# Two transformer blocks on one core: conditioning slots on other hosts, opening transfers reordered, second-half low parts on GpSimd

## What is computed

```python
# first block, for each of 2 layers
mod = silu(c) @ w_ada + b_ada                      # conditioning: 3 x 1024 values
shift, scale, gate = split(mod, 3)
h = rmsnorm(x, norm_g) * (1 + scale) + shift
rq, rk, rv, rg, xbc, dt, z, fq, fk, fv, fg, f = split(h @ w_in)
ret = rmsnorm(retention(rotary(rq), rotary(rk), rv)) * silu(rg)
xs, B, C = split(silu(causal_conv4(xbc)))
y = ssd_scan(xs, softplus(dt + dt_bias), -exp(a_log), B, C)    # then gated by z and normed
fox = causal_attention(fq, fk, fv, cumsum(log_sigmoid(f)))     # then gated by fg
x = x + gate * (concat(y, ret, fox) @ w_out)

# second block, for each of 2 layers, on latent and context positions (2 x 256; layer 1: latent only)
mod_x, mod_c = silu(c) @ ada_w + ada_b, silu(c_ctx) @ ada_w + ada_b     # 6 x 1024 values each
h = rmsnorm(x) * (1 + sc1) + sh1
conv = swish(layernorm(dwconv31(a * sigmoid(g)))) @ w_conv_out          # a, g: cua, cug
mlstm = bidirectional chunked mLSTM(mq, mk, mv, gates mg), normed, gated by mo, @ w_mlstm_out
att = grouped-query attention(aq, ak, av) @ w_attn_out
x = x + g1 * ((sigmoid(bg0) * conv + sigmoid(bg1) * mlstm + sigmoid(bg2) * att) @ w_out)
h = rmsnorm(x) * (1 + sc2) + sh2
u = dwconv3(h @ w_up)                                                   # upa, upg: 22 tiles each
x = x + g2 * ((u_a * silu(u_g)) @ w_down)
```

## Time and profile before

| | before |
|---|---|
| median of 3 runs | 2320.07 us |
| the profiled execution | 2319.95 us (span 2318.2 us) |
| PE busy | 2220.0 us, 96% |
| DVE busy | 1677.5 us, 72% |
| ACT busy | 978.7 us, 42% |
| POOL busy | 107.8 us, 5% |
| mean granted clock of TensorE | 0.983 |
| read from HBM | 321.29 MB |

### The profile page before, as it was taken

The page is one execution under the profiler, slowest core; times in us unless marked ns, Lnnn a source line. Parts: engine busy times, 40 slices in busy tenths (PEclk is TensorE's granted clock), DMA queues, the critical chain, the costliest instruction groups (busy, mean ns, idle before and its releaser), DMA issues.

```text
span 2318.2 us, 33297 instructions
## 1 busy us (share of the span) xinstructions
PE 2220.0 (96%) x13838; PEld 1886.0 (81%) x13838; DVE 1677.5 (72%) x3037; ACT 978.7 (42%) x1568; POOL 107.8 (5%) x86
## 2 busy tenths in 40 slices
PE   4999998999999999999999999999999999999999
PEld 3888887988877887778887677866778888998999
DVE  5897749877779776648734699976377767666984
ACT  3347643486523354453222333321244445644542
POOL 0000000000000022220000000000000222100000
PEclk9999999999999999999999999999999999999999
DMA  9883247533343111115522355544532212564553
GB/s 358 281 291 125 93 145 239 182 112 107 110 165 91 55 56 52 41 37 182 163 95 89 105 183 182 188 154 154 175 94 73 92 55 74 173 209 145 183 173 119
DMA packets 280807, 324.49 MB, mean 140 GB/s; under 512 B 28496, under 2 KB 261456, under 8 KB 280528
## 3 DMA queue, kind: packets, MB, share of 16 engines
q1 hardware_dynamic: 280656, 322.36, 42.3%
HBM read 321.29 MB, written 1.05 MB: 139 GB/s over the span
## 4 chain that ended last, share of the span: by engine, by line
PE 76%; DVE 18%; ACT 2%; DMA 2%; issue 1%; SPq 0%; POOL 0%; DVEq 0%; ACTq 0%
PE ps L732 74%; DVE ring L1886 3%; DVE parts L1928 2%; DVE ada_dot L1886 2%; DVE parts L2294 2%; DMA ring<-w_in 1%; DVE arena L2323 1%; ACT w_high L1390 1%; DVE arena L2657 1%; DVE arena L2659 1%; DVE arena L2027 1%; PE ps L1181 1%; DVE arena L2480 1%; DMA cols<-columns 1%; DVE arena L2072 0%
## 5 line engine op out<-in xcount | busy, mean ns | idle before, releaser
L732 PE MATMUL ps<-parts,w_high 128*128 128x256 f32 (+1 forms) x6512 | 1160.5, 328 | 12.8 <-issue 9.6
L732 PEld LDWEIGHTS ps<-parts,w_high 128*128 128x128 f32 x6512 | 977.6, 191 | 138.1 <-issue 24.3
L732 PE MATMUL ps<-parts,parts 128*128 128x256 f32 (+1 forms) x3384 | 618.3, 324 | 22.4 <-DVE parts L2294 11.9
L732 PEld LDWEIGHTS ps<-parts,parts 128*128 128x128 f32 x3384 | 507.4, 191 | 84.7 <-DVE parts L2294 17.3
L1390 ACT ACTIVATE w_high<-ring 128x1024 fp32r<-128x1024 f32 (+2 forms) x442 | 439.4, 1011 | 304.3 <-PE ps L732 171.7
L2294 DVE TENSOR_TENSOR parts<-ring,w_high 128x1024 fp32r<-128x1024 f32 (+2 forms) x282 | 320.5, 1142 | 141.4 <-ACT w_high L1390 141.1
L1886 DVE CUSTOM_DVE_ANT_0 ring<-ring,c_rows,cols 128x1024 f32<-128x1024 f32 x144 | 183.1, 1279 | 19.1 <-DMA ring<-w_ada_t 10.2
L732 PE MATMUL ps<-arena 128*64 128x256 f32 (+7 forms) x928 | 184.2, 396 | 11.3 <-ACT arena L1471 8.4
L1831 POOL TENSOR_TENSOR parts<-ring,w_high 128x512 fp32r<-128x512 f32 x80 | 107.4, 1368 | 1871.8 <-ACT w_high L1390 1871.7
L732 PEld LDWEIGHTS ps<-arena 128*128 128x128 f32 (+2 forms) x928 | 122.5, 171 | 59.5 <-issue 19.8
L2323 DVE SCALAR_TENSOR_TENSOR arena<-arena,cols 128x512 f32<-128x512 f32 (+1 forms) x240 | 159.5, 664 | 6.2
(11 more groups left out here) (266 smaller groups left out, 1854.7 us busy)
## 6 DMA issues: line engine op xcount, KB each, us to landing
ring<-w_in SPq DMA_DIRECT2D x118, 1024.0 KB, 5.1
ring<-ada_w_t SPq DMA_DIRECT2D x48, 1024.0 KB, 4.9
ring<-ffn_w_up SPq DMA_DIRECT2D x44, 1024.0 KB, 5.0
ring<-w_ada_t SPq DMA_DIRECT2D x24, 1024.0 KB, 7.0
ring<-w_out SPq DMA_DIRECT2D x16, 1024.0 KB, 5.1
ring<-ffn_w_down SPq DMA_DIRECT2D x16, 1024.0 KB, 5.3
ring<-w_out SPq DMA_DIRECT2D x16, 512.0 KB, 4.2
ring<-w_mlstm_out SPq DMA_DIRECT2D x8, 1024.0 KB, 5.1
```

The costliest lines, as they stand in the source:

```text
L732: return tensor.matmul(o, a, b, start=first, stop=last)
```

## The change

Five things are changed.

1. Other hosts (`conditioning_slots`). In the first block rv 1 of layer 0 becomes a host, xbc 0, 2 and 4 are no longer, and the first two slots of the output projection become hosts. In layer 1 the eight hosts are rv 1, fv 0, fv 1, rq 1, rk 1, fq 0, fk 0 and a slot of the output projection (before: rq 0 and xbc 1 in place of fk 0 and the last). In the second block the six slots of the conv and mLSTM projections that were hosts are none any more; nine bg and three bo slots carry what these and six bg slots carried. In the feed-forward stage the same twenty slots ride on upa and upg, but each step gets one with four tile products (on upg) and, but for two steps, one with two (on upa).
2. The opening: rv 0 is loaded ahead of the last two of the eight first conditioning slots; small and positions, the conditioning slot of rv 1 and rv 1 follow, and then the other parameter columns, constants and vectors. The waits for the other columns move to where they are read.
3. fv 0's tiles are computed ahead of the dt chain (in both layers).
4. The low parts of the second halves of rq, rk, xbc, fq and fk are computed by GpSimd (`one_lows`), 14 a layer, each as two instructions.
5. `weights_low_out` computes tiles of a host.

```diff
+FIRST_AHEAD = 6
 def conditioning_slots():
-    host(named(0, ("fv", 2), ("rq", 2), ("rk", 2), ("xbc", 6), ("fq", 2), ("fk", 2)), slots[1, 0][8:] + slots[1, 1])
-    host([("rv", 1, 1), ("fv", 1, 0), ("fv", 1, 1), ("rq", 1, 0), ("rq", 1, 1), ("rk", 1, 1), ("xbc", 1, 1), ("fq", 1, 0)], slots[2, 0][:8])
-    host([("cua", 0, 0), ("cug", 0, 1), ("cua", 0, 1), ("mk", 0, 0), ("mk", 0, 1), ("mk", 0, 2)], slots[2, 0][8:14])
-    host([("bg", 0, 0, 3)] + [("bg", 0, 1, s) for s in range(4)] + [("bg", 0, 2, 0)], slots[2, 0][14:20])
-    host([(part, 0, s) for s in range(1, 11) for part in ("upa", "upg")], slots[2, 0][20:] + slots[2, 1][:16])
+    odd = [("xbc", 0, s) for s in (1, 3, 5)]
+    host([("rv", 0, 1)] + named(0, ("fv", 2), ("rq", 2), ("rk", 2)) + odd + named(0, ("fq", 2), ("fk", 2)) + [("wo", 1, 0, s, 0) for s in range(2)],
+         slots[1, 0][8:] + slots[1, 1])
+    host([("rv", 1, 1), ("fv", 1, 0), ("fv", 1, 1), ("rq", 1, 1), ("rk", 1, 1), ("fq", 1, 0), ("fk", 1, 0), ("wo", 1, 1, 2, 0)], slots[2, 0][:8])
+    gates = [("bg", 0, n // 4, n % 4) for n in range(GATES_WHOLE, 12)]
+    host(gates + [("bo", 0, 2, s) for s in range(3)], slots[2, 0][8:20])
+    host([("upg", 0, s) for s in range(1, 11)], slots[2, 0][20:] + slots[2, 1][:6])
+    late = slots[2, 1]
+    host([("upa", 0, s) for s in range(1, 11)], late[8:10] + late[6:7] + late[10:13] + late[7:8] + late[13:16])
...
     first, hosts = conditioning_slots()
-    for slot in first:
+    main = main_slots(w)
+    for slot in first[:FIRST_AHEAD]:
         yield conditioning(slot)
-    for name, parts in main_slots(w):
+    yield next(main)
+    for slot in first[FIRST_AHEAD:]:
+        yield conditioning(slot)
+    for name, parts in main:
...
+SHARED_LOWS = ("rq", "rk", "xbc", "fq", "fk")
...
             load("c_row", c_row[:, 0, :], w["c_row"][0:1, :].to_broadcast([P, D]), "c_row")
+            load_slot(0)
             load("consts", cst[:, 0:N_FIRST], w["shape_consts"][:, 0:N_FIRST], "cst")
             load("row_0", cols[:, 1, :], w["columns"][:, 1, :], "row_0")
-            load_slot(0)
             load_slot(1)
             load("x_in", xT, w["x_t"], "x_in")
-            for n in range(2, RING):
+            for n in range(2, len(ada_first) + 1):
+                load_slot(n)
+            load("small", smalls[:, :], w["small"])
+            load("small", posi, w["positions"][0:1, :].to_broadcast([P, SEQ]), "small")
+            first_main = len(ada_first) + 1
+            for n in range(first_main, first_main + 2):
                 load_slot(n)
             load("rows", cols[:, 0, :], w["columns"][:, 0, :])
             load("rows", cols[:, 2:, :], w["columns"][:, 2:, :], "rows")
-            for n in range(RING, len(ada_first)):
-                load_slot(n)
-            load("small", ...)
-            load_slot(len(ada_first))
...
@@ GpSimd
+            def one_lows(l):
+                for n in range(half_no[("rq", l, 0), 0], half_no[("fk", l, 1), 1] + 1):
+                    (name, j), nk = split_halves[n], KT // 2
+                    if name[0] in SHARED_LOWS and j:
+                        p.wait_ge(*when(("w_high", n)))
+                        for part in (slice(0, nk), slice(nk, KT)):
+                            gpsimd.tensor_tensor(half_low(n)[:, part, :], half_raw(n)[:, part, :], half_high(n)[:, part, :].bitcast(F32), ALU.subtract).then_inc(*p.step(("w_low", n)))
+            for l in range(DEPTH):
+                one_lows(l)
@@ VectorE, weights_low
                         ada_tiles((part, l, s), j)
+                        if j and part in SHARED_LOWS:
+                            continue
...
-                ada_tiles(("rv", l, 1), 0)
-                ada_tiles(("rv", l, 1), 1)
+                for host in (("rv", l, 1), ("fv", l, 0)):
+                    ada_tiles(host, 0)
+                    ada_tiles(host, 1)
                 v.wait_ge(*when(("logs", l)))
...
-                for s in range(2):
-                    for j in range(2):
-                        ada_tiles(("fv", l, s), j)
+                ada_tiles(("fv", l, 1), 0)
+                ada_tiles(("fv", l, 1), 1)
...
                 def weights_low_out(n):
                     n += half_no[("wo", 1, l, 0, 0), 0]
+                    ada_tiles(*split_halves[n])
```

More of the change, by code:

```diff
@@ L197, in conditioning_slots @@
     named = lambda l, *parts: [(part, l, s) for part, n in parts for s in range(n)]
-    host(named(0, ("fv", 2), ("rq", 2), ("rk", 2), ("xbc", 6), ("fq", 2), ("fk", 2)), slots[1, 0][8:] + slots[1, 1])
-    host([("rv", 1, 1), ("fv", 1, 0), ("fv", 1, 1), ("rq", 1, 0), ("rq", 1, 1), ("rk", 1, 1), ("xbc", 1, 1), ("fq", 1, 0)], slots[2, 0][:8])
-    host([("cua", 0, 0), ("cug", 0, 1), ("cua", 0, 1), ("mk", 0, 0), ("mk", 0, 1), ("mk", 0, 2)], slots[2, 0][8:14])
-    host([("bg", 0, 0, 3)] + [("bg", 0, 1, s) for s in range(4)] + [("bg", 0, 2, 0)], slots[2, 0][14:20])
-    host([(part, 0, s) for s in range(1, 11) for part in ("upa", "upg")], slots[2, 0][20:] + slots[2, 1][:16])
-    host([("down", 0, s, part) for s in range(1, 4) for part in range(3)][:8], slots[2, 1][16:])
+    odd = [("xbc", 0, s) for s in (1, 3, 5)]
[7 more added lines that the diff above has]
+    host([("upa", 0, s) for s in range(1, 11)], late[8:10] + late[6:7] + late[10:13] + late[7:8] + late[13:16])
+    host([("down", 0, s, part) for s in range(1, 4) for part in range(3)][:8], late[16:])
     return first, hosts
@@ L688, in _ @@
             load("rows", cols[:, 2:, :], w["columns"][:, 2:, :], "rows")
-            for n in range(RING, len(ada_first)):
-                load_slot(n)
-            load("small", smalls[:, :], w["small"])
-            load("small", posi, w["positions"][0:1, :].to_broadcast([P, SEQ]), "small")
-            load_slot(len(ada_first))
             load("consts_2", cst[:, N_FIRST:], w["shape_consts"][:, N_FIRST:])
@@ L697, in _ @@
                 load("c_rows", c_row[:, vector, :], w["c_row"][vector:vector + 1, :].to_broadcast([P, D]), "c_rows")
-            for n in range(len(ada_first) + 1, len(slots)):
+            for n in range(first_main + 2, len(slots)):
                 if slots[n][0] == ("wo", 1, DEPTH - 1, 3, 1):
@@ L1405, in first_layer @@
                     scalar.activation((xconv if l else h1)[:, t, :], xT[:, t, :], ACT.Square).then_inc(*a.step(("sq1", l, t)))
-                if l == 0:
-                    a.wait_ge(*when("rows"))
                 rms_root(("ssq1", l), rms1[:, 0:SEQ // 4], D, ("root1", l), 0, SEQ // 4)
@@ L1418, in first_layer @@
                     scalar.activation(sinT, sinT, ACT.Sin).then_inc(*a.step("rope"))
+                    a.wait_ge(*when("rows"))
                 for s in range(2):
@@ L1914, in first_layer @@
                 v.wait_ge(*when("x_in"))
-                v.wait_ge(*when("rows"))
                 for t in range(KT):
@@ L1934, in first_layer @@
                     v.wait_ge(*when("small"))
+                    v.wait_ge(*when("rows"))
                     v.wait_ge(*when("cst"))
```

## The result

The changed kernel takes 2304.66 us (median of 9 runs, 2303.21 to 2316.18), the kernel before 2320.57 (9 runs beside them): ratio 0.995 with an interval of 0.9937 to 0.9964, so 0.5% faster and clear of no change. (The medians alone lie 0.7% apart; the ratio counts all runs, and the means are 2308.1 and 2320.5.) Six of the nine runs lie between 2303.2 and 2307.0 at a mean granted clock of 0.984 to 0.987, three between 2314.2 and 2316.2 at 0.978 and 0.979; the profiled one took 2306.98 (span 2305.2), 13.0 us of span less than the one before. The forecast was 2303. The total was met, but not by the steps that were to give it.

A forecast was written before the change was run, and what follows sets the result against it. TensorE, busy 2220.0 of 2318.2 us, was taken as the bound, waiting mainly for VectorE. First block's front and rq to fk -7.9, Part 4 -7.9, Part 5 -3.5, Part 6 +2.0: -17.3 from 2320.07, so 2303 us, range 2296 to 2310.

The forecast's parts named there:

- Part 1: Opening up to rq in layer 0: rq starts 5.2 us earlier, at 67.8 us (bounds 0 and 6).
- Part 2: rq to fk, layer 0: VectorE takes 77.5 us plus 28 GpSimd instructions' cost; the end comes at 170.5 us (-3.1).
- p: VectorE time lost per GpSimd instruction in rq to fk: taken as 0.9 us, bounds 0 to 1.40.
- Part 3: rq to fk, layer 1: VectorE 70.9 us of work plus 6 idle, plus GpSimd's cost; end at 454.0 us (-4.8).
- third rival: rq to fk: each GpSimd subtraction stops VectorE for its whole length; 2322 or 2331 us, chance 0.12.
- Part 4: Second block's conv and mLSTM projections: six hosts removed, TensorE's waits go, -7.9 us (bounds 0 and -9.6); branch stage 0.
- Part 5: Feed-forward of layer 0: heavy and light slots alternate, 6 tiles per step instead of 8; -3.5 us (bounds -2 and -3.5).
- Part 6: Output projection, both layers: added hosts cost +2 us (bounds 0 and +4), 1.2 in layer 0 and 0.8 in layer 1.
- The clock: Second block's projections: lower clock after the long wait, 0.77 granted in 730 to 740 us, 2.3 us of work.
- free GpSimd: rq to fk: GpSimd costs VectorE nearly nothing and TensorE is the bound in both layers; 2283 us, chance 0.25.
- stalls that return: Second block: stalls return elsewhere, branch stage delayed, feed-forward stays VectorE-bound; 2313 us, chance 0.13.
- the port rival: Same as the third rival: VectorE stopped throughout each GpSimd subtraction in rq to fk; 2322 or 2331 us, chance 0.12.

The follow-up runs named there:

- e4: Kernel before with only the new opening load order and fv 0's tiles ahead of the dt chain in both layers: 2310.18 us, ratio 0.996.
- e9: Kernel after with no rq-to-fk low parts on GpSimd, no conditioning slot ahead of rv 1, layer 0's hosts shifted later, last in output projection's fifth half: 2281.95 us.
- e2: Kernel before with only the 28 low parts of rq to fk moved to GpSimd: 2344.64 us, ratio 1.0109.
- e1: Kernel after with all low parts of rq to fk back on VectorE, the rest unchanged: 2292.13 us, ratio 0.9875.
- e10: Kernel after with the tiles of two layer 1 conditioning slots moved from fv 1 and rq 1 to xbc 1 and xbc 3: 2308.45 us, ratio 0.9958.
- e3: Kernel before with only the second block's hosts changed: 2301.77 us, ratio 0.993.

## Why the prediction was right in the sum and wrong in its parts

**Part 1, the front:** the order of events was right, one term mis-sized. "TensorE then needs 14.08 us for both fv slots": it took 15.57 at a lowered clock, and began at 54.95 instead of 53.2. With the full clock, and with one conditioning slot less ahead of it, rq starts at 67.75 (e4). "rq 0 has landed by then" was wrong too: the DMA queue delivered it at 68.2, behind one more conditioning slot; in the kernel after both limits lie close together, and e9 shows that taking away that slot alone gains nothing.

**Part 2, layer 0:** right. Forecast 77.5 + 25.2 = 102.7 us for the stretch, measured 103.0 (70.17 to 173.18); p forecast at 0.9 from the convolution steps of the second block, measured 0.89. The end is 2.7 us late, mostly because rq started 2.4 us late. "The moved subtraction thus saves 1.14 us and costs 1.8 us of the same engine" is what e2 and e1 show: 10 us more for layer 0 with the move alone, 10 less without it.

**Part 3, layer 1:** this step failed. VectorE's price was even lower than forecast (0.70), and TensorE was rid of the 5.42 us. But "with 6 us of idling as in layer 0" had VectorE idle for 6 us and it idled for 20.1: TensorE waited for GpSimd, the high-part buffers stayed full, and VectorE had nothing to do (7.74 us in one piece up to 377.24). So the stretch took 110.2 us in place of 102.1, 14.1 more of idling and 6.1 less of work; it also began 2.6 us later than forecast. I had asked what GpSimd costs VectorE, and not what VectorE costs GpSimd, though the prediction named "GpSimd's subtractions end late and TensorE waits for them" as what would make it wrong in its core. VectorE's run of four tiles, a low part, eight short subtractions and again tiles and a low part goes from 354.82 to 369.49 with no gap that the trace shows. GpSimd's first subtraction began at 355.32 and ended at 370.61, 1.1 us after that run; the second ended at 371.83, and TensorE went on at 371.88. e10 shows that it was this.

The Trainium skill, "SBUF — State Buffer", section "Who interferes with whom", says that issue order decides who blocks, and that the one that is second waits for the other's whole instruction. The rows agree that either engine can be the one kept out: a product of 3.42 us beside a GpSimd instruction that came first, and a GpSimd instruction of 15.29 us that came while a product was running. They differ from the rule's letter in the second case: by it GpSimd would have had its turn at 356.09, when that product ended, but 17 more VectorE instructions that began after 355.32 (the short reads of a sum not counted) went ahead of it. The prediction, its third rival too, used only one direction of the rule.

**Part 4** was right: -7.9 forecast, -8.5 measured, and e3 alone shows 8.7. The twelve hosts in the branch stage cost nothing, as taken. **Part 5** was too small, -5.0 against bounds of -2 and -3.5. The waits of 3.5 us went, and nearly all of the gain (4.9 us) comes at these five places, 0.7 to 1.1 us at each. The rows at the third of them, before and then after, show why the sum of the waits was too low a price:

```profile
1396.01 3.89 PE L732 MATMUL ps<-parts,w_high 128*128 128x512 f32 x16
1400.68 2.13 PE L732 MATMUL ps<-parts,parts 128*128 128x512 f32 x8 [0.77 <-DVE parts L2294]
```

```profile
1390.05 3.89 PE L744 MATMUL ps<-parts,w_high 128*128 128x512 f32 x16
1393.77 2.03 PE L744 MATMUL ps<-parts,parts 128*128 128x512 f32 x8
```

From start to start it is 4.67 us before and 3.72 after, 0.95 us, while the idle time is given as 0.77: it counts from the end of the last matmul, and without a wait the next one starts before that end.

**Part 6** was right in size, +2 forecast; layer 0 cost 2.3, since the second tile also delays the chain that TensorE waits for, and layer 1 nothing.

**The clock** was priced behind one wait only. Up to the copy of layer 1 the kernel after spends 13.6 us more at 1.2 GHz than the one before, so at most 6.8 us of the miss there are the clock's. It is not the long wait that makes the difference: 6.8 us at 1.2 GHz follow from 369 us on, when TensorE had been idle since 364.9, but the kernel before has as many from 363 us on, behind its wait of 5.42 us. Behind that copy the kernel after spends 17.0 us less. So the first block came out 11.9 us worse than forecast and the second 7.6 better, which no step had foreseen. That the two cancel but for 4.3 us, and the total was met, is luck. **The rivals:** free GpSimd and stalls that return are both refuted; the port rival has the sign of the move alone right (e2 is slower by 25 us), but not its price: at 1.25 us an instruction layer 0 would have lost 28 x 1.25 - 16.0 = 19.0 us, and it lost 10.1.

## What to carry to other kernels

Before work goes to a second engine that shares a port, price both directions: what the busy engine loses per instruction, and how long the helper stands behind the busy engine's longest unbroken run when its result is due. Split a mixed change into its parts and time them: here 17.9 and 9.4 us of gain stood beside a loss of 12.5 us (e1) that the total hid. And where two versions differ by less than 0.5%, compare the granted clock in the part that both share before crediting the edit.

## What the runs showed of the hardware

- VectorE's tile product, whose collisions no row of before showed, is blocked like the others: 1.27 us alone, 2.32 beside a GpSimd subtraction of 1.25 that came first, 3.42 beside one of 2.49.
- GpSimd can be kept out over many VectorE instructions: 15.29 us for one subtraction of 1.25, until 1.1 us after the end of the run, while each VectorE instruction ran at its full speed (1.27 us for a tile product). Where GpSimd had come first, the two took turns (two subtractions in 3.63 us, the products between them 2.32 and 2.31). What makes it a run in one case and turns in the other is open.
- Programs that are the same from some 440 or 465 us on spent 31 to 62 us of that part at 1.2 GHz, each in one profiled execution.
